# Depthwise convolution of eight tiles: from five on TensorE and three on VectorE to four and four, with shifted copies moved from VectorE and ScalarE to transfers, and the channel means summed on GpSimd

## The reference, cut to what matters

```python
def conformer_conv(h, n_seg, w_pw1, b_pw1, w_dw, b_dw, ln_g, ln_b, w_pw2, b_pw2):
    B, L, D = h.shape                       # 1, 512, 1024
    u = h @ w_pw1 + b_pw1                   # 1024 -> 2048
    a, gate = jnp.split(u, 2, axis=-1)
    u = a * jax.nn.sigmoid(gate)            # GLU
    u = dwconv(u.reshape(B * n_seg, L // n_seg, D), w_dw).reshape(B, L, D) + b_dw   # 31 taps, 8 segments of 64
    u = jax.nn.silu(layer_norm(u, ln_g, ln_b))      # mean and variance over the 1024 channels
    return u @ w_pw2 + b_pw2
```

## Time and profile before

| | |
|---|---|
| time, median of 3 runs | 2232.72 us (2231.89 to 2236.44) |
| the profiled execution | 2232.25 us, its span 2230.5 us |
| PE busy | 2167.7 us, 97% of the span |
| DVE, ACT, POOL busy | 44%, 18%, 3% |
| convolution stage | 37.1 to 198.1 us of the span |

### The profile page before, as it was taken

One profiled execution on the slowest core, in us unless ns is written; L12 is line 12 of the kernel. 1 busy time (PEld: TensorE's weight loads), 2 busy tenths in 40 slices (PEclk: granted clock), 3 DMA queues, 4 the chain that ended last, 5 costly groups with the idle time before them and its releaser, 6 DMA issues.

```text
span 2230.5 us, 25164 instructions
## 1 busy us (share of the span) xinstructions
PE 2167.7 (97%) x10268; PEld 1316.1 (59%) x10268; DVE 990.0 (44%) x1436; ACT 397.4 (18%) x784; POOL 68.9 (3%) x89
## 2 busy tenths in 40 slices
PE   7999999999999999998999999999999899999999
PEld 3343488878886777865544444436888644444443
DVE  3883297788855643843122222125555322222222
ACT  3214222002113121852100000002000200000000
POOL 1100100000012000001000000001000000000000
PEclk9999999999999999998999999999999899999999
DMA  9416334567650112032799999996212499999997
GB/s 351 157 44 232 108 135 167 203 250 265 226 208 10 67 38 90 1 151 113 322 429 428 428 428 429 429 426 256 75 76 80 201 420 428 428 429 428 429 429 303
DMA packets 107036, 564.24 MB, mean 253 GB/s; under 512 B 8904, under 2 KB 17614, under 8 KB 79310
## 3 DMA queue, kind: packets, MB, share of 16 engines
q1 hardware_dynamic: 106528, 563.03, 62.8%
q10 hardware_dynamic: 430, 0.13, 0.0%
HBM read 561.04 MB, written 2.10 MB: 252 GB/s over the span
## 4 chain that ended last, share of the span: by engine, by line
PE 85%; DMA 10%; DVE 3%; ACT 1%; issue 1%; SPq 0%; POOL 0%; DVEq 0%; ACTq 0%
PE psum L1643 22%; PE psum L2108 17%; PE psum L2092 8%; PE psum L1382 8%; DMA ring<-in_moe_w_down_dram 6%; PE psum L2200 5%; PE psum L1791 4%; PE psum L2146 4%; PE psum L1815 3%; PE psum L1972 2%; DMA ring<-in_mlp_w_dram 2%; PE psum L1948 2%; PE psum L1923 2%; PE psum L1590 2%; PE psum L1539 1%; DMA ring<-in_moe_w_up_dram 1%
## 5 line engine op out<-in xcount | busy, mean ns | idle before, releaser
L2108 PE MATMUL psum<-ring,arena 128*64 128x512 f32 x2048 | 445.2, 593 | 5.1 <-DMA ring<-in_moe_w_up_dram 5.1
L2108 PEld LDWEIGHTS psum<-ring,arena 128*64 128x64 f32 x2048 | 144.8, 137 | 300.1 <-issue 286.1
L2092 PE MATMUL psum<-ring,arena 128*64 128x512 f32 x768 | 224.8, 594 | 2.1 <-DMA ring<-in_moe_w_down_dram 2.1
L3000 DVE TENSOR_TENSOR arena<-psum,arena 128x512 f32<-128x512 f32 x32 | 33.9, 1059 | 385.9 <-PE psum L2108 385.9
L1382 PE MATMUL psum<-hT,ring 128*128 128x512 f32 x416 | 180.6, 593 | 3.0 <-ACT hT L905 3.0
L1643 PE MATMUL psum<-ring 128*128 128x256 f32 x640 | 142.9, 380 | 4.6 <-DVE rstd L2583 4.6
L1643 PE MATMUL psum<-hT,ring 128*128 128x256 f32 x608 | 139.3, 386 | 0.8 <-ACT hT L899 0.8
L1382 PEld LDWEIGHTS psum<-hT,ring 128*128 128x128 f32 x416 | 78.6, 190 | 101.6 <-issue 96.9
L1643 PEld LDWEIGHTS psum<-ring 128*128 128x128 f32 x640 | 121.0, 190 | 24.4 <-issue 8.3
L2146 PEld LDWEIGHTS psum<-arena 128*128 128x128 f32 x1024 | 121.4, 198 | 14.0 <-issue 14.0
L1643 PEld LDWEIGHTS psum<-hT,ring 128*128 128x128 f32 x608 | 117.4, 194 | 18.6 <-issue 2.2
(11 more groups left out here) (415 smaller groups left out, 2580.4 us busy)
## 6 DMA issues: line engine op xcount, KB each, us to landing
ring<-in_moe_w_gate_dram SPq DMA_DIRECT2D x64, 2048.0 KB, 19.1
ring<-in_moe_w_up_dram SPq DMA_DIRECT2D x64, 2048.0 KB, 16.4
ring<-in_moe_w_down_dram SPq DMA_DIRECT2D x44, 2048.0 KB, 20.7
ring<-in_ada_w_dram SPq DMA_DIRECT2D x24, 2048.0 KB, 9.0
ring<-in_mlp_w_dram SPq DMA_DIRECT2D x16, 2048.0 KB, 8.5
hT<-in_moe_w_down_dram SPq DMA_DIRECT2D x16, 2048.0 KB, 14.7
ring<-in_w_mod_dram SPq DMA_DIRECT2D x12, 2048.0 KB, 12.6
ring<-in_conv_w_in_dram SPq DMA_DIRECT2D x6, 2048.0 KB, 19.4
```

Source lines behind the costliest of these rows:

```text
L2092: ins = pe.matmul(psum[64 * e:64 * e + 64, bank + nh, :], src[:, 4 * h + k, 64 * e:64 * e + 64], w[:, k, nh * N:(nh + 1) * N], start=h == ...
L2108: ins = pe.matmul(psum[64 * nh:64 * nh + 64, bank + e, :], src[:, 4 * h + k, 64 * e:64 * e + 64], w[:, k, nh * N:(nh + 1) * N], start=h == ...
```

## The change: four tiles each, shifts by transfers, means by sums

1. Tile 0 goes from PE to DVE: `PE_CONV` is (2, 4, 6, 7), `DVE_CONV` (0, 1, 3, 5). A fourth set of tap columns is loaded, so the taps are turned into two tiles instead of one.
2. `glu(j)` is one product on 128 partitions into a zero-padded row buffer `glu_row` (736 elements a partition, laid over the two buffers of the norm's root). The 16 shifted copies of a tile (four r, four c, 32 partitions by 736 - r elements each) are transfers from `glu_row` to `urep`. ACT issues all 16 for the first three tiles; for tile 7, ACT issues eight and SP eight. SP waits for these in its list, behind the first block of `mod_gemv(2)` and the small loads, ahead of the other blocks. `glu` waits until the tile before it was copied.
3. POOL adds the seven tiles 0 to 6 as they come (six additions into `cv_sum`), and PE makes two products, of `cv_sum` and of `cv` 7.
4. PE's order is pw1(0), turn of the taps, pw1(1), pw1(2), pw1(3), conv(2), pw1(4), pw1(5), conv(4), pw1(6), pw1(7), mod_gemv(1), conv(6), conv(7), turn, the two means. DVE's order is own 0, glu 2, own 1, glu 4, own 3, own 5 with glu 6 in its middle, glu 7.

```diff
-PE_CONV = (0, 2, 4, 6, 7)
-DVE_CONV = (1, 3, 5)
+PE_CONV = (2, 4, 6, 7)
+DVE_CONV = (0, 1, 3, 5)
+MEANS = (0, 2, 1, 3, 4, 5, 6)
+MEAN_AT = ((1, 2), (3, 4, 5, 6))
...
+        glu_row = carve(roots, 0, SEGS * SEGP)
+        cv_sum = carve(K, KCOL["um"][0], N)
...
+        def shifted_copy(queue, m, r, c):
+            u = carve(arena, m % 2 * UREP, SHIFTS, SEGS * SEGP)
+            queue.dma_start(u[32 * r:32 * r + 32, c, 0:SEGS * SEGP - r], glu_row[32 * c:32 * c + 32, r:SEGS * SEGP])\
+                .then_inc(S[f"u_spread{m % 2}"], 16)
...
+                if n == B_MOD[2][0]:
+                    sp.wait_ge(S["u_ready"], 4)
+                    sp.wait_ge(S["tile_done"], T_CV[PE_CONV[1]] + 1)
+                    for r in range(2):
+                        for c in range(SHIFTS):
+                            shifted_copy(sp, 3, r, c)
...
+            def mean_add(i):
+                for j in MEANS[0:2] if i == 1 else MEANS[i:i + 1]:
+                    if j in PE_CONV:
+                        pool.wait_ge(*emptied(T_CV[j])(0))
+                    else:
+                        pool.wait_ge(S["conv_done"], DVE_CONV.index(j) + 1)
+                if i > 1:
+                    pool.wait_ge(S["mean_sum"], i - 1)
+                pool.tensor_tensor(cv_sum, cv[:, MEANS[0], :] if i == 1 else cv_sum, cv[:, MEANS[i], :], ALU.add)\
+                    .then_inc(S["mean_sum"], 1)
...
                 pool.tensor_tensor(taps[m % 2], stack, w, ALU.mult).then_inc(S["taps_ready"], 1)
+                if m >= 2:
+                    for i in MEAN_AT[m - 2]:
+                        mean_add(i)
...
-                act.wait_ge(S["u_base"], m + 1)
-                for r in (2, 3):
+                act.wait_ge(S["u_ready"], m + 1)
+                if m >= 2:
+                    act.wait_ge(S["tile_done"], T_CV[PE_CONV[m - 2]] + 1)
+                for r in range(2 if m == 3 else 0, SHIFTS):
                     for c in range(SHIFTS):
-                        ins = act.activation(u[32 * r:32 * r + 32, c, :, PAD - r:PAD - r + SEG],
-                                             u[0:32, c, :, PAD:PAD + SEG], ACT.Copy)
-                ins.then_inc(S["u_spread"], 1)
+                        shifted_copy(act, m, r, c)
...
-            for m in range(4):
-                pw1(2 * m)
-                spread(m)
-                pw1(2 * m + 1)
-                conv_out(2 * m)
-                if m == 3:
-                    spread(4)
-            mod_row(1)
+            pw1(0)
+            pw1(1)
+            for m in range(3):
+                pw1(2 * m + 2)
+                spread(m)
+                pw1(2 * m + 3)
+                if m == 2:
+                    spread(3)
+                    mod_row(1)
+                conv_out(2 * m + 2)
...
+            def conv_mean():
+                pe.wait_ge(S["rms_ready"], 1)
+                pe.wait_ge(S["mean_sum"], len(MEANS) - 1)
+                pe.matmul(psum[:, STAT, :], const("ones_d"), cv_sum, start=True, stop=False)
+                pe.wait_ge(*emptied(T_CV[DT - 1])(0))
+                pe.matmul(psum[:, STAT, :], const("ones_d"), cv[:, DT - 1, :], start=False, stop=True)\
+                    .then_inc(S["mean_done"], 1)
...
             def glu(j):
                 m = PE_CONV.index(j)
                 dve.wait_ge(*emptied(T_PW1[j])(1))
+                if m:
+                    dve.wait_ge(S[f"u_spread{(m - 1) % 2}"], 16 * SHIFTS * SHIFTS * ((m - 1) // 2 + 1))
+                a, s, u = (x.rearrange("p (s w) -> p s w", s=SEGS) for x in (glu_a[:, j % 2, :], glu_s[:, j % 2, :], glu_row))
+                dve.tensor_tensor(u[:, :, PAD:PAD + SEG], a, s, ALU.mult).then_inc(S["u_ready"], 1)
...
+                        if between is not None and k == TAPS // 2:
+                            glu(between)
...
+            link(dve.memset(glu_row, 0.0))
+            own_conv(0)
+            glu(2)
+            own_conv(1)
+            glu(4)
+            own_conv(3)
+            own_conv(5, 6)
+            glu(7)
```

More of the change, by code:

```diff
@@ L151, in block_kernel @@
         if j == 0:
-            T_TAPS = tiles(["dve"])
-        if j % 2:
+            T_TAPS = tiles(["dve"] * 2)
+        if j % 2 and j > 1:
             T_CV[j - 1] = tiles(["act"])
@@ L283, in block_kernel @@
         sq = sb("sq", [P, 2, N])
-        rms = sb("rms", [P, N])
-        rstd = sb("rstd", [P, N])
+        roots = sb("roots", [P, 2 * N])
+        rms, rstd = roots[:, 0:N], roots[:, N:2 * N]
         tmp = sb("tmp", [P, 2, N])
@@ L441, in block_kernel @@
             "n_ms", "n_inv", "n_wide", "half_scaled", "half_ready", "late_sq",
-            "u_base", "u_ready", "u_spread", "u_own", "conv_done", "mean_done", "mean_sb", "centered",
+            "u_ready", "u_spread0", "u_spread1", "u_own", "conv_done", "mean_sum", "mean_done", "mean_sb", "centered",
             "x_pw2", "gains", "hid_ready", "mlp_wsum", "mlp_wsum4", "mlp_tsum", "mlp_part", "mlp_m1", "mlp_read",
@@ L772, in _ @@
                 elif m == 0:
-                    pool.wait_ge(*emptied(T_TAPS)(0))
+                    pool.wait_ge(*emptied(T_TAPS)(1))
                     pool.wait_ge(S["sq_used"], DT)
@@ L1593, in conv @@
                 ins.then_inc(S["tile_done"], 1)
[L1595 to L1618, removed]
+            def conv_mean():
[5 more added lines that the diff above has]
+                    .then_inc(S["mean_done"], 1)
+            pw1(0)
+            pe.wait_ge(S["taps_in"], 16 * N_TAPS)
+            pe.wait_ge(S["tap_pad"], 1)
+            for m in range(2):
+                turn_tile(T_TAPS + m, [(vec_rows[0:VEC_ROWS[g], g, :], VEC_ROWS[g]) for g in (2 + 2 * m, 3 + 2 * m)])
+            pw1(1)
+            pw1(2)
+            pw1(3)
+            conv(2)
+            pw1(4)
+            pw1(5)
+            conv(4)
+            pw1(6)
+            pw1(7)
+            mod_gemv(1)
+            conv(6)
             conv(7)
             mod_turn(1)
-            conv_mean(6)
-            conv_mean(7).then_inc(S["mean_done"], 1)
+            conv_mean()
             pe.wait_ge(S["mean_sb"], 1)
@@ L2414, in glu, with own_conv @@
                 m = PE_CONV.index(j)
-                u = urep[m % 2]
                 dve.wait_ge(*emptied(T_PW1[j])(1))
[L2417 to L2428, removed]
+                if m:
+                    dve.wait_ge(S[f"u_spread{(m - 1) % 2}"], 16 * SHIFTS * SHIFTS * ((m - 1) // 2 + 1))
+                a, s, u = (x.rearrange("p (s w) -> p s w", s=SEGS) for x in (glu_a[:, j % 2, :], glu_s[:, j % 2, :], glu_row))
+                dve.tensor_tensor(u[:, :, PAD:PAD + SEG], a, s, ALU.mult).then_inc(S["u_ready"], 1)
+            def own_conv(j, between=None):
                 m = DVE_CONV.index(j)
+                if m:
+                    dve.wait_ge(S["conv_done"], m)
                 dve.wait_ge(*emptied(T_PW1[j])(1))
@@ L2447, in own_conv @@
                 ins.then_inc(S["conv_done"], 1)
-            dve.wait_ge(S["tile_done"], T_TAPS + 1)
             for g in range(2, 6):
-                w = VEC_ROWS[g]
-                ins = dve.tensor_copy(vecT[:, g * P:g * P + w], psum[:, T_TAPS % 6, (g - 2) * P:(g - 2) * P + w])
-                if g < 5:
+                w, t = VEC_ROWS[g], T_TAPS + g // 2 - 1
+                dve.wait_ge(S["tile_done"], t + 1)
+                ins = dve.tensor_copy(vecT[:, g * P:g * P + w], psum[:, t % 6, g % 2 * P:g % 2 * P + w])
+                if g % 2:
+                    ins.then_inc(FREE["dve"], 1)
+                else:
                     link(ins)
-            ins.then_inc(FREE["dve"], 1)
-            dve.wait_ge(*emptied(T_TAPS)(0))
+            dve.wait_ge(*emptied(T_TAPS)(1))
             link(dve.memset(upad[:, :, 0:PAD], 0.0))
             link(dve.memset(upad[:, :, PAD + SEG:UPAD], 0.0))
[L2459 to L2463, removed]
+            dve.wait_ge(S["scaled"], DT)
+            link(dve.memset(glu_row, 0.0))
+            dve.wait_ge(S["pads_zero"], 5)
+            own_conv(0)
[5 more added lines that the diff above has]
+            glu(7)
             dve.wait_ge(S["mean_sb"], 1)
```

15 lines of the change are left out of this document (7 added, 8 removed).

## The result

| | before | changed |
|---|---|---|
| time, median of 4 runs each, us | 2234.4 (2231.89 to 2236.44) | 2221.81 (2217.92 to 2223.73) |
| ratio, with its 95% interval | | 0.9946 (0.9934 to 0.9958) |
| the profiled execution, us (its span) | 2232.25 (2230.5) | 2217.92 (2216.1) |
| first product of the stage begins | 37.11 | 37.35 |
| ACT copies the mean | 198.07 | 187.98 |

The account below looks back on a forecast made before the run. PE, busy 97% of the span, was taken to bound the kernel. 12.4 us leaving PE less 0.7 us of waiting gives 11.7 us: 2220.55 against the profiled execution, 2221.0 us as median, range 2219.0 to 2227.0.

Parts of the forecast that it names:

- What leaves PE: Convolution stage: one convolution (7.00 us) and six mean products (5.75 us) leave PE; 12.4 us gained if PE never waits.
- VectorE's chain: Convolution stage, VectorE: glu(2) ends at 82.6, glu(4) at 115.5, glu(6) at 156.6 and glu(7) at 170.3 us.
- The copies: Shifted copies: a tile takes 8.9 us on one queue; first three tiles hidden, conv(7) waits 0.7 us (0 to 9).
- I take 0.45: Shifted copies: one issue was taken to cost 0.45 us, from rows of 0.33, 0.48 and SyncE's 0.63.
- two queues issue in 3.6 us, so the data rate limits: Tile 7's copies: data takes 5.1 us plus 1.65, landing at 177.0 when PE is ready at 176.4.
- its own case: The forecast's case before conv(7): conv(7) at most 1.5 us late; chance 0.55.
- the signs set down: Stage: means done near 186, everything behind 11 to 12 us earlier, 16 copies landing about 9 us after glu.
- Behind the stage everything is released by PE's progress: After the stage: the MLP's waits for weights move along with PE and give nothing back.
- (a): Copies: narrow pieces get half the transfer rate, 215 GB/s; tile 7 lands 2.6 us late, 2222.9 us; chance 0.22.
- (b): Copies: slow at 125 GB/s, 13.7 us a tile; conv(2), conv(4), conv(7) wait, 2231.8 us; chance 0.08.
- (c): Copies: each waits for the landing ahead, 33.6 us a tile; slower than before, 2274.6 us; chance 0.07.
- (d): Weight loads: SyncE held until 179, blocks at 331 GB/s, fourth block 3 to 4 us late; 2224.5 us; chance 0.03.

Follow-up runs that it names:

- e7: Changed kernel with glu(6) and glu(7) moved inside VectorE's last own convolution, before its taps 8 and 25: 2219.54 us, ratio to before 0.9934.
- e2: Changed kernel with GpSimd's third and fourth addition made to wait until VectorE's last own convolution is done: 2221.64 us.
- e3: Changed kernel with each copy moving only the first half of its columns, same count of copies, old data in the rest: 2218.07 us.
- e5: Kernel before with the means alone changed: GpSimd adds tiles 0 to 6, PE makes two mean products instead of eight: 2235.22 us, ratio 1.0006.
- e11: Kernel before with six of its eight mean products left out and no additions on GpSimd, the mean being of two tiles only: 2230.71 us.
- e8: Changed kernel with all sixteen copies of tile 7 issued by ScalarE, SyncE's loads held until those copies have landed: 2225.91 us.
- e1: Changed kernel with all sixteen copies of tile 7 issued by ScalarE, none by SyncE, whose loads are no longer held: 2238.07 us.
- e4: Changed kernel with the copies made as before, by eight products on VectorE and eight activations on ScalarE, no transfers: 2232.34 us, ratio to before 0.9999.

## Why the prediction was right

**What leaves PE: right.** 12.4 us were worked out from durations in the earlier trace rows; the stage shows 12.38 with the waits added, and e7, which has none before conv(7), 12.4.

**VectorE's chain: right** to within 0.5 us for three of the four products; glu(2) came 1.1 us earlier than its estimate (own 0 runs from 54.05 to 80.80, so the two tap sets beside it cost some 2 us, not 3.0). The additions' price, scaled from the tap sets in the earlier trace rows, was 1.76 us for two; e2 shows 1.71. Half an addition beside glu(7) was counted too and did not come: glu(7) took 0.68 us, and it was GpSimd's addition (second line, in GpSimd's order of time) that took 1.66 us where two took 3.18 and the last, alone, 1.26:

```profile
142.30 3.18 POOL L792 TENSOR_TENSOR K<-K,arena 128x512 f32<-128x512 f32 x2 [4.56 <-DVE arena L2474]
169.55 1.66 POOL L792 TENSOR_TENSOR K<-K,arena 128x512 f32<-128x512 f32 x1 [24.07 <-DVE arena L2474]
```

**The copies: the mechanism right, the size off.** The mis-sized term is the issue, "I take 0.45": 0.64 us on one queue, 0.67 and 0.72 on two, above every row used for it but SyncE's 0.63, the only one from a long series of issues. So a tile on one queue took 11.9 us, not 8.9, and the 1.7 us that conv(2) was to have to spare became a wait of 0.19; conv(4) and conv(6) had cover enough. For tile 7, "two queues issue in 3.6 us, so the data rate limits" failed in the same way, though not wholly, as e3 shows 1.6 us that do hang on the bytes: the issues took 5.8 us, the last copies landed 2.7 us later (SP's last issue ended at 175.87, conv(7) started at 178.57), together 8.5 where 6.75 were forecast, and the wait was 1.86 instead of 0.7, beyond the 1.5 us that the forecast allowed for its own case. Net: 10.3 us of the stage, not 11.7. So of the signs set down, the means were ready at 187.9, not near 186, what follows came 10.1 us earlier, not 11 to 12, and a tile's copies were there 11.9 us after glu, not 9.

**Why the time came out close all the same.** That the median lies 0.8 us from the forecast, with 1.4 us too much counted in the stage, is luck. Part of the gain came from outside the stage. From the spreading of the norm ahead of the MLP (`token_widen`, 275 us in the kernel before) to the last sums behind it (`x_stat`) the kernel before and its variants e5 and e11 take 412.9, 417.1 and 414.8 us, the changed kernel and the nine others 409.9 to 412.0: no overlap, though the nearest two are only 0.9 us apart, and nothing of it was forecast. In the two profiled executions, before and changed, the difference is 2.3 us, and nearly all of it stands in PE's waits on VectorE there, 4.64 against 2.49 us; the longest of them, before and then changed:

```profile
500.92 3.69 PE L1643 MATMUL psum<-ring 128*128 128x256 f32 x16 [3.19 <-DVE rstd L2583]
```

```profile
489.67 3.69 PE L1676 MATMUL psum<-ring 128*128 128x256 f32 x16 [2.08 <-DVE roots L2619]
```

So the step "Behind the stage everything is released by PE's progress" doesn't hold whole: something there gave time back, and why VectorE is less late was not tested. The medians of the two series of runs, 12.6 and 9.1 us faster, lie on both sides of the forecast 11.7.

**Rivals.** (a) *Half the transfer rate* would have given conv(7) a wait of 2 to 4 us, and 1.86 lies just short. The cause is another: on one queue halving the bytes leaves the issuing as it was and brings the landing 0.2 us forward (e3), on two it gives back 1.6 us, where the slices of the transfer view read up to 254 GB/s before the loads start, against 146 to 151 on one. The rule weighed with it, from the Trainium skill (SBUF — State Buffer, "Can I just issue two DMAs to hit both halves?"), that a second transfer at the same time gains 6%, does not carry over to a second queue for these copies: from glu to conv(7) it is 8.5 us with two queues and 12.4 in e8 with one (171.17 to 183.57), as one queue is held by its issues. What two large transfers at once would gain no run here shows. The Trainium skill also says (DMA: Bandwidth & Descriptors, Issuing engines are not separate DMA queues) that several issuing engines save only the sequencer's time, usually small; here that saving is what the second queue brings, but it is not small: for a tile's sixteen copies on one queue the issues are 10.2 of 11.9 us. (b) and (c), slow copies or copies in sequence: no; sixteen landed in 11.9 us, not 13.7 or 33.6. (d) SyncE was released at 175.9, 2 us later than forecast, and neither mod_gemv(2) nor the second product waited.

**What no rival had**: what would happen if the loads ran beside the copies (e1). The order of SP's list kept it from happening, and the forecast counted that order only as a risk for the loads.

## What to carry to other kernels

Work taken off a bound engine is a gain only as far as the engine that takes it over has room just there: two of the additions cost the changed order 1.1 us (e2), and the additions took back 4.5 of 5.0 us in the old one (e5 against e11). Price a series of small transfers by its issues, from a row of a series like it, before its bytes. And read the place of a transfer in a queue's list also as a barrier for what stands behind it: taking eight copies out of SP's list let 2 MB loads run into the rest, and that alone cost 13.4 us of the stage (e1 against e8).

## What the runs showed of the hardware that was not expected

- An issue of a 32-partition copy inside SBUF takes about 0.64 us whether it carries 92 KB or 46 KB (for sixteen, 10.23 and 10.24 us at the first tile, 10.14 and 10.14 at the third). Whether fewer and larger copies would issue faster no run tested.
- Beside 2 MB loads such a copy lands after 4.2 to 8.7 us (medians of its four lengths, e1); with the loads held it is 2.2 (e8).
- A wait of PE can cost more than itself: a convolution of 7.07 us takes 8.77 after a wait of 2.78 us, 9.14 after 4.69, 8.71 after 5.77, 10.04 after 11.02 and 8.76 after 12.10, while after 1.86 it is 7.07. The granted clock, 1.00 in the changed kernel, is 0.91 and 0.70 in those windows of e1, and 0.75 and 0.76 in e4's (176.7 to 188 and 188 to 205 us). It need not: behind a wait of 2.97 us pw1(0) of the changed kernel ran at 1.00.
